# Attention as one row of 32 query blocks, with a block's output matmuls placed behind the turning of the next block

## What is computed

```python
# differential attention (twice): 8 heads, 2 maps each, 128 queries at a time, keys up to the block's end
for s0 in range(0, seq, QBLOCK):
    e = s0 + QBLOCK
    s = jnp.einsum('bhmqd,bhmkd->bhmqk', q[:, :, :, s0:e], k[:, :, :, :e]) * scale
    p = _chunk_causal_softmax(s, s0)
    wts = p[:, :, 0] - lam * p[:, :, 1]
    outs.append(jnp.einsum('bhqk,bhkd->bhqd', wts, v[:, :, :e]))
# latent attention (once): one map, scores are the sum of two products, keys up to the block's end
# attention over 768 keys (once)
def gqa_block(q, k, v):
    s = jnp.einsum('bqkgd,bskd->bkgqs', q, k) * (HEAD_DIM ** -0.5)
    p = jax.nn.softmax(s, axis=-1)
    return jnp.einsum('bkgqs,bskd->bqkgd', p, v)
```

## Time and profile before

| what | us |
|---|---|
| median of 3 runs | 4035.24 |
| lowest, highest | 4032.95, 4039.49 |
| the profiled execution, its own time | 4035.5 |
| its span in the trace | 4033.7 |
| PE busy | 3461.4 (86%) |
| DVE busy | 1811.5 (45%) |
| ACT busy | 1229.6 (30%) |
| four attention cores, first T to last O | 447.2 |

### The profile page before, as it was taken

One profiled execution on the slowest core, in us unless ns is written; L12 is line 12 of the kernel. 1 busy time (PEld: TensorE's weight loads), 2 busy tenths in 40 slices (PEclk: granted clock), 3 DMA queues, 4 the chain that ended last, 5 costly groups with the idle time before them and its releaser, 6 DMA issues. The chain is left out here.

```text
span 4033.7 us, 43128 instructions
## 1 busy us (share of the span) xinstructions
PE 3461.4 (86%) x16316; PEld 2627.1 (65%) x16316; DVE 1811.5 (45%) x2791; ACT 1229.6 (30%) x2137; POOL 62.6 (2%) x74
## 2 busy tenths in 40 slices
PE   7977897787799669897978988889999896789998
PEld 5855665524578443486867855678888753547886
DVE  4545595324363656684243469342222304314333
ACT  3244322343332522473212212232111203523222
POOL 0000000001000000000000002000000000000000
PEclk9988999989999989898989999899999998999999
DMA  3211211200121221492012121111111110012221
GB/s 133 84 43 52 84 42 42 89 22 4 74 92 57 49 98 63 178 371 83 24 42 84 42 93 53 63 63 63 63 63 58 37 42 22 0 63 94 94 94 63
DMA packets 47511, 289.94 MB, mean 72 GB/s; under 512 B 6903, under 2 KB 7159, under 8 KB 15960
## 3 DMA queue, kind: packets, MB, share of 16 engines
q1 hardware_dynamic: 46936, 286.63, 20.2%
q0 software_dynamic: 448, 1.57, 0.1%
HBM read 265.10 MB, written 14.68 MB: 69 GB/s over the span
## 5 line engine op out<-in xcount | busy, mean ns | idle before, releaser
L398 PE MATMUL bank<-high,slot_high 128*128 128x512 f32 x3280 | 1204.8, 367 | 147.7 <-DVE low L327 103.7
L399 PE MATMUL bank<-low,slot_high 128*128 128x512 f32 x3280 | 1194.4, 364 | 0.0
L400 PE MATMUL bank<-high,slot_low 128*128 128x512 f32 x3280 | 1187.1, 362 | 0.0
L378 DVE TENSOR_TENSOR slot_low<-slot,slot_high 128x2048 fp32r<-128x2048 f32 (+1 forms) x162 | 366.7, 2265 | 1157.4 <-ACT slot_high L372 1157.0
L398 PEld LDWEIGHTS bank<-high,slot_high 128*128 128x128 f32 x3280 | 623.6, 190 | 269.8 <-issue 145.9
L372 ACT ACTIVATE slot_high<-slot 128x2048 fp32r<-128x2048 f32 (+1 forms) x162 | 306.6, 1893 | 1328.0 <-PE bank L400 1105.4
L400 PEld LDWEIGHTS bank<-high,slot_low 128*128 128x128 f32 x3280 | 622.1, 190 | 100.1
L399 PEld LDWEIGHTS bank<-low,slot_high 128*128 128x128 f32 x3280 | 624.1, 190 | 96.1 <-issue 4.3
L795 DVE TENSOR_REDUCE peak<-bank 128x1 f32<-128x128 f32 (+2 forms) x224 | 110.2, 508 | 268.5 <-PE bank L920 105.4
L852 ACT ACTIVATE prob<-bank,peak_bias 128x128 f32<-128x128 f32 (+2 forms) x224 | 119.5, 539 | 121.4 <-DVE peak_bias L803 120.9
L435 PE MATMUL bank<-slot_high,high 128*128 128x256 f32 x448 | 128.1, 286 | 27.3 <-DVE low L325 27.3
(11 more groups left out here) (337 smaller groups left out, 4239.5 us busy)
## 6 DMA issues: line engine op xcount, KB each, us to landing
mod_raw<-in_mod SPq DMA_DIRECT2D x48, 1024.0 KB, 6.5
slot<-in_gu SPq DMA_DIRECT2D x44, 1024.0 KB, 5.0
slot<-in_a_in SPq DMA_DIRECT2D x32, 1024.0 KB, 4.9
slot<-in_e_rest SPq DMA_DIRECT2D x16, 1024.0 KB, 5.0
slot<-in_down SPq DMA_DIRECT2D x16, 1024.0 KB, 4.9
spectra<-f_spectrum SPq DMA_DIRECT2D x12, 1024.0 KB, 3.8
h_spectrum<-spectra SPq DMA_DIRECT2D x12, 1024.0 KB, 5.0
slot<-in_a_out SPq DMA_DIRECT2D x8, 1024.0 KB, 5.2
```

Of the source, the lines that this page charges most:

```text
L378: dve.tensor_tensor(k.slot_low[s][:, 0:n], k.slot[s][:, 0:n], k.slot_high[s][:, 0:n].bitcast(F32), ALU.subtract).then_inc(k.low[s], 1)
L398: pe.matmul(out, wh, xh, start=kt == 0, stop=False)
L399: pe.matmul(out, wh, xl, start=False, stop=False)
L400: mm = pe.matmul(out, wl, xh, start=False, stop=kt == self.kt - 1)
```

## The change

The loop of four turns is gone: all 32 blocks x are written out, in one row, with fixed addresses and fixed semaphore values. S, K and E of blocks 8, 9, 16, 17, 24 and 25 now stand at the same distance ahead as all others. O(x-1) and take(x-1) stand behind T(x), or behind S(x+2) where there is one map, and behind E(x+2). In the wide attention the second piece of T goes into bank 7, into one half of it by x's parity, so it no longer waits for the first piece's copy. The small tiles `peak`, `peak_bias`, `total` and `inv_total` get 64 columns instead of 16.

```diff
-            for x, (c, n) in enumerate(self.pieces(self.keys[q])):
-                per = 2 if self.wide else 1
-                pe.wait_ge(k.drained[b], u.free(b, i * (4 * per) + ((j // 2) * per + x)))
+            for piece, (c, n) in enumerate(self.pieces(self.keys_of(x))):
+                at = 0
+                if piece == 0:
+                    pe.wait_ge(k.drained[b], u.free(b, x // 2))
+                else:
+                    b, at = 7, (x % 2) * 256
+                    pe.wait_ge(k.drained[7], u.free(7, x))
                 for c2 in range(0, n, P):
...
-        def outputs(i, j):
...
+        def outputs(x):
+            (i, hh), b = divmod(x // 4, 2), self.t_bank(x)
+            pe.wait_ge(k.drained[b], u.full(b, x // 2))
+            if self.wide:
+                pe.wait_ge(k.drained[7], u.full(7, x))
+            pe.wait_ge(k.drained[6], u.free(6, x))
...
-        def turn(i):
-            scores(i, 0)
-            scores(i, 1)
-            for j in range(8):
-                if j + 2 < 8 and self.maps == 2:
-                    scores(i, j + 2)
-                turn_probs(i, j)
-                if j + 2 < 8 and self.maps == 1:
-                    scores(i, j + 2)
-                outputs(i, j)
...
-        loop(pe, 4, turn)
+        scores(0)
+        scores(1)
+        for x in range(self.BLOCKS):
+            if x + 2 < self.BLOCKS and self.maps == 2:
+                scores(x + 2)
+            turn_probs(x)
+            if x + 2 < self.BLOCKS and self.maps == 1:
+                scores(x + 2)
+            if x:
+                outputs(x - 1)
+        outputs(self.BLOCKS - 1)
...
+        peak(0)
+        peak(1)
+        for x in range(self.BLOCKS):
+            mix(x)
+            if x + 2 < self.BLOCKS:
+                peak(x + 2)
...
-            for j in range(8):
-                evacuate(i, j)
-                if j + 2 < 8:
-                    exp(i, j + 2)
-                take(i, j)
-
-        loop(act, 4, turn)
+        exp(0)
+        exp(1)
+        for x in range(self.BLOCKS):
+            evacuate(x)
+            if x + 2 < self.BLOCKS:
+                exp(x + 2)
+            if x:
+                take(x - 1)
+        take(self.BLOCKS - 1)
```

More of the change, by code:

```diff
@@ L691, in close @@
             u.add([b], 16)
-        u.add([4, 5], 16 * (2 if self.wide else 1))
+        u.add([4, 5], 16)
         u.add([6], 32)
+        if self.wide:
+            u.add([7], 32)
     def pieces(self, n):
@@ L735, in scores @@
             if self.wide:
[L736 to L740 removed]
+                for b, (c, m) in zip(self.s_banks(x), self.pieces(n)):
+                    self.score(pe, hh, 0, q, c, m, k.ps[b], True).then_inc(k.filled[b], 1)
+            else:
+                for m, b in zip(range(self.maps), self.s_banks(x)):
@@ L788, in vector, with peak @@
         chain = k.named("mix_step")
[L790 to L795, removed]
+        def peak(x):
+            n_b = len(self.s_banks(x))
+            for y, b in enumerate(self.s_banks(x)):
+                n = self.pieces(self.keys_of(x))[y][1] if self.wide else self.keys_of(x)
+                dve.wait_ge(k.filled[b], u.full(b, x // 2))
+                ins = dve.tensor_reduce(self.peak[:, 2 * x + y:2 * x + y + 1], k.ps[b][:, 0:n], AX.X, ALU.max)
@@ L830, in turn @@
-        def turn(i):
-            peak(i, 0)
-            peak(i, 1)
-            for j in range(8):
-                mix(i, j)
-                if j + 2 < 8:
-                    peak(i, j + 2)
-        loop(dve, 4, turn)
+                    dve.tensor_tensor(self.total[:, first], self.total[:, first], self.total[:, second], ALU.add)\
+                       .then_inc(mixed.sem, 1)
+                    dve.wait_ge(mixed.sem, mixed.at(x + 1))
+                dve.reciprocal(self.inv[:, first], self.total[:, first]).then_inc(inv.sem, 1)
@@ L856, in evacuate, with exp @@
-        def evacuate(i, j):
-            b, q = self.t_bank(j), j % 4
-            for x, (c, n) in enumerate(self.pieces(self.keys[q])):
-                act.wait_ge(k.filled[b], u.full(b, i * (4 * per) + ((j // 2) * per + x)))
-                act.activation(self.turned[j % 2][:, c:c + n], k.ps[b][:, 0:n], ACT.Copy).then_inc(k.drained[b], 1)
-        def take(i, j):
-            hh, q = divmod(j, 4)
-            act.wait_ge(k.filled[6], u.full(6, i * 8 + j))
-            out = cols(self.out, i * (self.order[0] * P) + (q * D + hh * self.order[1] * P), P)
+        def exp(x):
+            act.wait_ge(biased.sem, biased.at(x + 1))
+            for y, b in enumerate(self.s_banks(x)):
+                c, n = self.pieces(self.keys_of(x))[y] if self.wide else (0, self.keys_of(x))
+                m = 0 if self.maps == 1 else y
+                one = 2 * x if self.wide else 2 * x + y
+                act.activation(self.prob[x % 2][m][:, c:c + n], k.ps[b][:, 0:n], ACT.Exp,
+                               bias=self.bias[:, one:one + 1], scale=self.scale,
+                               accum_out=self.total[:, 2 * x + y:2 * x + y + 1]).then_inc(k.drained[b], 1)
@@ new lines, in evacuate, with take @@
+        def evacuate(x):
+            b = self.t_bank(x)
+            for piece, (c, n) in enumerate(self.pieces(self.keys_of(x))):
+                at, use = 0, x // 2
+                if piece:
+                    b, at, use = 7, (x % 2) * 256, x
+                act.wait_ge(k.filled[b], u.full(b, use))
+                act.activation(self.turned[x % 2][:, c:c + n], k.ps[b][:, at:at + n], ACT.Copy).then_inc(k.drained[b], 1)
+        def take(x):
+            (i, hh), q = divmod(x // 4, 2), x % 4
+            act.wait_ge(k.filled[6], u.full(6, x))
+            at = i * (self.order[0] * P) + (q * D + hh * self.order[1] * P)
+            out = self.out[:, at:at + P]
```

109 lines of the change are left out of this document (43 added, 66 removed).

## The result

The changed kernel takes **3923.41 us** (median of four, 3922.14 to 3936.69) against 4036.06 for the kernel before, measured beside it: a ratio of 0.9728 (95% interval 0.9706 to 0.9751). The forecast was 3924.

What follows compares the result with a forecast made beforehand. Bound: a chain of handovers, no engine filling the attention cores. Gains of 55.4 (wide), 22.2 and 22.5 (differential) and 11.1 (latent) sum to 111.2 us, from the median 4035.2 to 3924; range 3907 to 3954.

Steps and rivals of the forecast that it cites:

- Wide attention: Bank wait goes and TensorE itself bounds: 3.36 us a block, 105.1 against 160.50, gain 55.4 us.
- the margin of take: Wide attention: the chain through K, E and take is ready 0.57 us before O(x) is due.
- rival (a): Wide attention: take behind E becomes the bound, 0.5 us more a block, 16 us back, 3940; chance 0.2.
- Latent attention: TensorE's 7.9 plus a 1.25 us wait for take: 9.2 per four blocks, 74.0 against 85.13, gain 11.1 us.
- Differential attentions: Four blocks in 9.8 us instead of 11.52, each stage 78.4 us; gains 22.2 and 22.5 us.
- VectorE's own 9.2: Differential attentions: VectorE's own work for four blocks, 8.76 us busy, 9.2 with short gaps between dependent steps.
- The waits of K: Differential attentions: VectorE's waits for scores, 0.6 us in four blocks, added to 9.2 for a 9.8 period.
- take(4) behind E(7) makes O(5) some 0.4 late: Differential attentions: delay hidden by VectorE's M(7); without that cover it would cost up to 0.4 us in four blocks.
- Seams: Between turns all engines run empty; removal counted as 8.4 us in the first differential stage, nearly all of latent's 11.1.
- (b): Only seams and the bank wait go; S still comes late for VectorE in the differential stages: 3953; chance 0.1.
- (c): Slower instruction supply, every block having its own code: 2.0 us for each of 128 blocks, 4180; chance 0.04.
- (d): The change doesn't do what it says, O's held by something else; time stays within 0.2%; chance 0.02.

Runs made afterwards that it cites:

- the kernel with O ahead of T: Changed kernel, differential attentions only: O(x-1) ahead of T(x) on TensorE and take(x-1) ahead of V(x) on ScalarE; 3904.72 us, ratio 0.9666.
- the work taken off VectorE: Changed kernel with M of the differential attentions leaving out the scaling of the first map; 3922.81 us, ratio 0.9725.
- the take moved ahead of E: Changed kernel, differential attentions only: take(x-1) ahead of E(x+2) on ScalarE instead of behind it; 3916.13 us, ratio 0.9693.
- the kernel with one row alone: Changed kernel with O(x) and take(x) back in their old places and T's second piece in its old bank; 3992.87 us, ratio 0.9888.
- the kernel with one row and bank 7: Changed kernel with O(x) and take(x) back where they stood before, bank 7 kept; 3951.44 us, ratio 0.9788.
- the seams written out: Kernel before, written out without a loop, old order and banks, row still emptied at every eighth block; 4023.48 us, ratio 0.9967.

## Why the prediction was right, step by step

**Wide attention: right.** 105.34 against 105.1, the margin of take held (rival (a) would have shown O waiting in each block; there are two such waits, 1.2 us in all). The period is 3.29 and not 3.36, since six transposes in one group take 0.65 and not 0.73; the 2.3 us that this gives are spent at the two ends, for which I had put 0.2.

**Latent attention: right.** 73.1 against 74.0, the wait 1.14 against 1.25, the period 9.02 against 9.2.

**Differential attentions: the gain was 4 us too large in each**, 82.1 and 83.1 against 78.4, and the period of 9.93 against 9.8 is right for a wrong reason. Two steps failed there and nearly made up for each other. First, "VectorE's own 9.2" was read from a stretch that held waits inside its groups: the K of 1.20 us for two banks (and again above) takes 1.01 when both banks are ready, in the kernel with O ahead of T (row below). There four blocks take 8.96 with a wait of 0.17, so VectorE's own is at most 8.79. The waits of K that the prediction added to it were nearly right: 0.28 + 0.33 + 0.17 = 0.78 in the rows of the change, against 0.6. Second, "take(4) behind E(7) makes O(5) some 0.4 late; VectorE has M(7) to do meanwhile, so this is hidden" was wrong: the work taken off VectorE gave nothing back and the take moved ahead of E gave 8.5 us. The prediction had bounded what this could cost at 0.4 in four blocks, and the period did shorten by 0.30; the size was right and "hidden" was not. I had walked along VectorE once and added up its waits, but hadn't asked whether a loop without VectorE's M is longer. The third part is the clock, for which the sum had no term at all (next section). 8 x 9.93 = 79.4; the other 2.7 us of 82.1 are clock and ends.

VectorE's K of a three-tile block in the kernel with O ahead of T:

```profile
264.83 1.01 DVE L804 TENSOR_REDUCE peak<-bank 128x1 f32<-128x384 f32 x2
```

**Seams: undersized.** I had some 33 us for them in all; the kernel with one row alone gives 36 in the cores and 44.6 by the medians. The stretches between the cores run the same code in all these kernels. The one between the third and the fourth attention takes 1964 to 1977 us in the profiled executions, so several us of the difference between two executions are scatter.

**The total** of 3923.4 against 3924.0 is thus closer than its terms: the cores gave 103.6 us in the first profile and 105.6 in the second, not 111.2. The other 7 us came from outside the cores in the medians, where the change does nothing that a row shows. Outside its cores the profiled execution before took 3586.5 us, and the other thirteen, the change among them, took 3576 to 3591, so 7 us is within the scatter there. That the forecast was hit to 0.6 us is luck; by the cores alone the gain was 6 to 8 us smaller than the sum.

**Rivals.** (a) would have shown a period near 3.9 in the wide attention; it is 3.29. (b) would have kept the period near 11.5, and the kernel with one row and bank 7 is that case, 3951.4 against the 3953 given for it. (c) fell with the seams written out; its price had a landing at 2.0 us at least, where the earlier trace rows has 1.9 as the shortest and 2.0 as the median. (d) fell with the waits.

## What to carry to other kernels

When one engine's own work seems to set a period, look for the loop: follow one block's scores through every queue, with what stands ahead in each, until the same engine is at the same step again, and compare the sum with the engine's own work. A step that is put behind another in one engine's queue (take behind E) ties it to that one's inputs, and before a step is moved in one queue, look at what its partner in the other queue stands behind: the same order on TensorE gave 20 us with take moved ahead too and lost 48 without. And a group's duration that covers two waits for two banks isn't work: take it from a stretch where nothing is waited for.

## What the runs showed of the chip that I had not expected

TensorE's granted clock depends on the order of the work inside such a stage. In the changed kernel it falls soon after a stretch in which TensorE had little to do, from the full 2.4 GHz to 1.2 GHz (0.50), for some 3 us at the beginning of the first differential attention and for the rest of it at its end. Windows of the first differential attention, its beginning and its end (columns as in the earlier trace rows; the clock is the third number from the right):

```profile
250.00:252.00 2.00, 0.93 (x6) 0.72 (x7) 1.90 (x8) 2.00 (x9) 0.00 (x0) 1.00 0.47 109
252.00:254.00 2.00, 2.00 (x10) 1.66 (x9) 1.58 (x4) 1.08 (x7) 0.00 (x0) 0.66 0.49 110
254.00:256.00 2.00, 2.00 (x9) 1.83 (x9) 0.98 (x6) 1.55 (x6) 0.00 (x0) 0.50 0.02 5
...
320.00:322.00 2.00, 0.20 (x3) 0.19 (x3) 1.65 (x6) 1.67 (x6) 0.00 (x0) 1.00 0.00 0
...
324.00:328.29 4.29, 3.57 (x18) 3.01 (x15) 0.00 (x0) 1.13 (x4) 0.00 (x0) 0.54 0.00 0
```

What it costs can be read where two stages run the same code. With one row and bank 7 the first differential attention takes 92.84 us and the second 89.49:

```profile
246.00:338.84 92.84, 72.43 (x357) 49.19 (x356) 67.49 (x214) 61.47 (x245) 0.00 (x0) 0.96 0.15 35
...
1304.67:1394.16 89.49, 69.08 (x357) 46.41 (x356) 67.45 (x214) 61.55 (x247) 0.00 (x0) 1.00 0.16 37
```

VectorE and ScalarE are busy for the same time; only TensorE takes longer, at 0.96 of the clock instead of 1.00, and the stage with it by 3.4 us. With O ahead of T both stages stand at 1.00 and take 8 x 8.96 + 0.2 us; the change, at 0.95, has 2.7 us beside its eight periods. The order with the shortest waits thus gained twice in these executions: the waits, and the slow us. But not every wait brings a fall. The wait of 1.35 us that each later period of the change has ahead of T(6) left the clock at 1.00 (9.93 us, the window in the result), and the kernel with take ahead of E, with the same wait, had 1.00 and 0.97 in its two stages. Nor does the fall belong to the code alone: the changed kernel run again had 0.98 in the first differential stage (80.4 us) and 0.95 in the second (82.8). The first four blocks of the first stage, in the execution profiled first and in the second one, show what it costs there:

```profile
246.15:257.06 10.91, 9.08 (x39) 6.33 (x38) 8.55 (x29) 7.31 (x29) 0.00 (x0) 0.84 0.21 48
```

```profile
247.05:256.35 9.30, 7.53 (x40) 5.03 (x38) 8.37 (x28) 7.13 (x29) 0.00 (x0) 0.99 0.25 56
```

The same code takes 1.6 us longer where the clock was at 0.84. What decides when the clock falls stays open here.
